# Prompt attention of a streaming encoder step: values as the stationary operand, two heads side by side, and the reciprocal row sums put into the transposition

## The reference

```python
admissible = key_chunk[None, :] <= (pb // CHUNK)[:, None]          # CHUNK = 64
score = jnp.einsum('bth,bths->bts', wb.astype(F32), jax.nn.relu(dots))
sel_val, sel_idx = lax.top_k(jnp.where(admissible[None], score, -jnp.inf), n_sel)   # 256 keys
...
logits = jnp.einsum('btkgd,btskd->btkgs', qg, kg, preferred_element_type=F32) * scale
logits = jnp.where(valid[:, :, None, None, :], logits, -jnp.inf)
p = jax.nn.softmax(logits, axis=-1).astype(vg.dtype)
o = jnp.einsum('btkgs,btskd->btkgd', p, vg)
```

## Time and profile before

| | us |
|---|---|
| median of 3 runs | 4250.42 |
| lowest and highest run | 4244.04, 4252.89 |
| span of the profiled execution | 4256.5 |
| prompt attention in it, first row maximum to last output | 646.3 |
| of this, tiles 0 to 3 | 207.0 |
| of this, tiles 4 to 7 and the end | 439.3 |

### The profile page before, as it was taken

How to read it: one execution, slowest core, us unless ns; L and a number is a source line. 1 busy time by engine, 2 the same in 40 slices (tenths; PEclk the granted TensorE clock), 3 DMA queues, 4 the chain that set the end, 5 groups by cost and what they waited for, 6 DMA issues and landing times. The chain is left out here.

```text
span 4256.5 us, 57639 instructions
## 1 busy us (share of the span) xinstructions
PE 3965.5 (93%) x20761; PEld 3571.6 (84%) x20777; DVE 2283.6 (54%) x3818; ACT 1126.7 (26%) x2017; POOL 220.7 (5%) x300
## 2 busy tenths in 40 slices
PE   6999999987999999979978899999888899999998
PEld 5988888876999999969963678888447799999997
DVE  5455555545444444454477888877223444444445
ACT  4322222213111111122133433333332311112111
POOL 2000000003000000020000000000000200000000
PEclk8888888869999999999958555555999999999999
DMA  2111011001111111111212000000431011111111
GB/s 85 36 36 36 32 36 37 31 11 42 40 45 36 50 40 40 42 42 66 74 44 84 16 6 6 1 1 1 175 148 40 27 40 45 45 36 46 40 45 57
DMA packets 58083, 187.32 MB, mean 44 GB/s; under 512 B 6960, under 2 KB 23344, under 8 KB 53488
## 3 DMA queue, kind: packets, MB, share of 16 engines
q1 hardware_dynamic: 53184, 165.22, 11.2%
q0 software_dynamic: 4656, 18.65, 1.4%
HBM read 164.28 MB, written 19.57 MB: 43 GB/s over the span
## 5 line engine op out<-in xcount | busy, mean ns | idle before, releaser
L205 PE MATMUL ff0lin<-ff0h_hi,ff0w_hi 128*128 128x384 f32 x1056 | 356.1, 337 | 23.7 <-POOL ff0h_lo L163 15.4
L205 PE MATMUL ff1lin<-ff1h_hi,ff1w_hi 128*128 128x384 f32 x1056 | 356.7, 338 | 21.7 <-POOL ff1h_lo L163 13.8
L206 PE MATMUL ff1lin<-ff1h_lo,ff1w_hi 128*128 128x384 f32 x1056 | 356.1, 337 | 0.0
L207 PE MATMUL ff1lin<-ff1h_hi,ff1w_lo 128*128 128x384 f32 x1056 | 355.6, 337 | 0.0
L206 PE MATMUL ff0lin<-ff0h_lo,ff0w_hi 128*128 128x384 f32 x1056 | 355.2, 336 | 0.0
L207 PE MATMUL ff0lin<-ff0h_hi,ff0w_lo 128*128 128x384 f32 x1056 | 354.8, 336 | 0.0
L1643 PEld LDWEIGHTS ap_bank<-at_v,ap_probs_t 128*128 128x128 f32 x1152 | 258.6, 331 | 36.4 <-ACT ap_probs_t L1688 20.4
L205 PE MATMUL hg_lin<-hg_h_hi,hg_w_hi 128*128 128x384 f32 x768 | 271.1, 353 | 16.1 <-POOL hg_h_lo L163 14.2
L1643 PE MATMUL ap_bank<-at_v,ap_probs_t 128*128 128x64 f32 x1152 | 269.1, 418 | 10.2 <-ACT ap_probs_t L1688 10.1
L206 PE MATMUL hg_lin<-hg_h_lo,hg_w_hi 128*128 128x384 f32 x768 | 265.0, 345 | 0.0
L207 PE MATMUL hg_lin<-hg_h_hi,hg_w_lo 128*128 128x384 f32 x768 | 264.4, 344 | 0.0
(11 more groups left out here) (328 smaller groups left out, 8767.4 us busy)
## 6 DMA issues: line engine op xcount, KB each, us to landing
ff0raw<-in_weights SPq DMA_DIRECT2D x66, 512.0 KB, 3.3
ff1raw<-in_weights SPq DMA_DIRECT2D x66, 512.0 KB, 3.2
hg_raw<-in_weights SPq DMA_DIRECT2D x40, 512.0 KB, 3.3
as_keys<-in_cache_k SPq DMA_DIRECT2D x16, 1024.0 KB, 4.8
as_vals<-in_cache_v SPq DMA_DIRECT2D x8, 2048.0 KB, 9.2
pj_raw<-in_weights SPq DMA_DIRECT2D x18, 512.0 KB, 3.9
se_keys<-in_cache_ki SPq DMA_DIRECT2D x8, 1024.0 KB, 4.7
x<-in_x SPq DMA_DIRECT2D x3, 1536.0 KB, 7.1
```

The lines of the kernel that those rows point to most:

```text
L205: pe.matmul(out, w_hi, x_hi, start=start, stop=False)
L206: pe.matmul(out, w_hi, x_lo, start=False, stop=False)
L207: return pe.matmul(out, w_lo, x_hi, start=False, stop=stop)
```

## The change

The two heads of a block become one unit, and the pipeline has one more stage. Per unit:

- Scores: the products of the two heads alternate, so that neighbours use partitions 0 to 63 and 64 to 127. For tiles 4 to 7 the second piece of keys stands behind the first half's transposition of the unit before.
- q is negated when it is projected and the mask is +1e30, so VectorE takes a minimum, and the exponential has scale -1; the negation (L1754) is gone. The minima of both heads are joined in one instruction.
- The row sums of both heads are inverted in one instruction, and it now stands behind the unit's top steps instead of ahead of them.
- GpSimd multiplies the identity by the two columns of reciprocals (`diag`, new, 128 x 256). The transposition becomes a float32 product with `probs` stationary and `diag` moving, which transposes and scales at once.
- Values: V (64 columns) is stationary, `probs_t` (128 columns) moving. The two heads write partitions 0 to 63 and 64 to 127 of one bank. The output comes out transposed, so L1649, `o` and L1702 are gone, and one copy of 128 x 128 per unit is left.
- `probs` and `probs_t` hold two units, q has one buffer. In `attend_sample_phase` the negation of the maximum and the drain ahead of it are gone.

```diff
-NEG = -1e30
+NEG = 1e30
...
-                    copy_rows(m * 2 + (Q_SLAB + par), m * 2 + (FIRST_Q + par), 1 - par, HEAD_D ** -0.5)
+                    copy_rows(m * 2 + (Q_SLAB + par), m * 2 + (FIRST_Q + par), 1 - par, -HEAD_D ** -0.5)
...
+            def diagonal(n):
+                pool.wait_ge(inv_set, n + 1)
+                if n >= 2:
+                    pool.wait_ge(turned, 2 * parts_before[n - 1])
+                pool.tensor_tensor(diag[:, n % 2], spread(const["ident"][:, :].unsqueeze(1), [P, 2, P]),
+                                   spread(inv[:, n % 2], [P, 2, P]), ALU.mult).then_inc(diag_set, 1)
+            split_lo(0)
+            for n in range(n_units):
+                if n % QB == QB // 2 and n // QB + 1 < PT:
+                    split_lo(n // QB + 1)
+                diagonal(n)
...
         @block.tensor
+            def scores(n, c):
+                t, j = units[n]
+                if c >= len(parts[n]):
+                    return
+                if j == 0 and c == 0:
                     pe.wait_ge(q_lo_set, t + 1)
                 if n:
-                    pe.wait_ge(maxed, 2 * n + half - 1)
-                for c, (a, e) in enumerate(pieces((t + 1) * P)):
-                    out, keys = qk[half][c][:, 0:e - a], (rows, j // GROUP, slice(a, e))
-                    pe.matmul(out, q_hi[rows, t % 2, j, :], k_hi[keys], start=True, stop=False)
-                    pe.matmul(out, q_lo[rows, t % 2, j, :], k_hi[keys], start=False, stop=False)
-                    i = pe.matmul(out, q_hi[rows, t % 2, j, :], k_lo[keys], start=False, stop=True)
+                    pe.wait_ge(read, parts_before[n - 1] + min(c + 1, len(parts[n - 1])))
+                a, e = parts[n][c]
+                for q_part, k_part in ((q_hi, k_hi), (q_lo, k_hi), (q_hi, k_lo)):
+                    for half in range(2):
+                        rows = slice(half * HEAD_D, (half + 1) * HEAD_D)
+                        i = pe.matmul(qk[half][c][:, 0:e - a], q_part[rows, t % 2, j, :], k_part[rows, j // GROUP, a:e],
+                                      start=q_part is q_hi and k_part is k_hi, stop=k_part is k_lo)
                 i.then_inc(qk_done, 1)
             def turn(n, half):
-                t, j = blocks[n]
-                pe.wait_ge(exped, 2 * n + half + 1)
-                if n or half:
-                    pe.wait_ge(turned_out, 2 * n + half)
+                pe.wait_ge(diag_set, n + 1)
+                for c, (a, e) in enumerate(parts[n]):
+                    m = turn_no(n, half, c)
+                    if m >= 2:
+                        pe.wait_ge(turned_out, m - 1)
+                    for k in range(a // P, e // P):
+                        i = pe.matmul(tr[m % 2][:, (k * P - a):(k * P - a) + P], probs[:, n % 2, half, k * P:(k + 1) * P],
+                                      diag[:, n % 2, half, :], start=True, stop=True)
+                    i.then_inc(turned, 1)
+            def values(n):
+                t, j = units[n]
+                pe.wait_ge(turned_out, 2 * parts_before[n + 1])
+                if n >= 2:
+                    pe.wait_ge(o_out, n - 1)
+                out = ob[n % 2]
                 for c in range(t + 1):
-                    i = pe.transpose(tr[c // 4][:, c % 4 * P:(c % 4 + 1) * P], probs[:, half, c * P:(c + 1) * P], const["ident"][:, :])
-                i.then_inc(turned, 1)
...
+                    for half in range(2):
+                        col = (j // GROUP * 2 + half) * HEAD_D
+                        i = pe.matmul(out[half * HEAD_D:(half + 1) * HEAD_D, 0:P], v_sb[:, c, col:col + HEAD_D],
+                                      probs_t[:, n % 2, half, c * P:(c + 1) * P], start=c == 0, stop=c == t)
                 i.then_inc(pv_done, 1)
...
+            for n in range(n_units + 2):
+                if n < n_units:
+                    scores(n, 0)
+                if 0 <= n - 1 < n_units:
+                    turn(n - 1, 0)
+                if n < n_units:
+                    scores(n, 1)
+                if 0 <= n - 1 < n_units:
+                    turn(n - 1, 1)
+                if n >= 2:
+                    values(n - 2)
...
+                act.activation(probs[:, n % 2, half, 0:keys], probs[:, n % 2, half, 0:keys], ACT.Exp, bias=low[:, n % 2, half],
+                               scale=-1.0, accum_out=total[:, n % 2, half]).then_inc(exped, 1)
+                act.activation(o_t[:, j, t * P:(t + 1) * P], ob[n % 2][:, 0:P], ACT.Copy).then_inc(o_out, 1)
...
+            def invert(n):
+                dve.wait_ge(exped, 2 * n + 2)
+                if n >= 2:
+                    dve.wait_ge(diag_set, n - 1)
+                dve.reciprocal(inv[:, n % 2], total[:, n % 2]).then_inc(inv_set, 1)
+            def minima(n):
+                t = units[n][0]
+                one = len(parts[n]) == 1
+                if n >= 2:
+                    dve.wait_ge(turned, 2 * parts_before[n - 1])
+                for c, (a, e) in enumerate(parts[n]):
+                    dve.wait_ge(qk_done, parts_before[n] + c + 1)
+                    for half in range(2):
+                        i = dve.tensor_tensor_reduce(out=probs[:, n % 2, half, a:e], in0=qk[half][c][:, 0:e - a],
+                                                     in1=mask_p[:, mask_at(t) + a:mask_at(t) + e], scale=1.0, scalar=3e38,
+                                                     op0=ALU.add, op1=ALU.min,
+                                                     accum_out=low[:, n % 2, half] if one else part_min[:, n % 2, c, half:half + 1])
+                    i.then_inc(read, 1)
+                if one:
+                    dve.drain().then_inc(low_set, 1)
+                else:
                     dve.drain()
...
+                    dve.tensor_tensor(low[:, n % 2], part_min[:, n % 2, 0].unsqueeze(2), part_min[:, n % 2, 1].unsqueeze(2),
+                                      ALU.min).then_inc(low_set, 1)
+            for n in range(n_units):
+                minima(n)
+                take_top(steps_by[n - 1] if n else first_steps, steps_by[n])
+                invert(n)
...
-                dve.reduce_max(neg_max[:, p], part_max[:, p, :], AX.X)
-                dve.drain()
-                dve.tensor_scalar(neg_max[:, p], neg_max[:, p], -1.0, None, ALU.mult).then_inc(maxed, 1)
+                dve.tensor_reduce(low[:, p], part_min[:, p, :], AX.X, ALU.min).then_inc(maxed, 1)
```

170 lines of the change are left out of this document (59 added, 111 removed).

## The result

| | before | after |
|---|---|---|
| median of 7 runs, us | 4250.12 (4244.04 to 4253.5) | 4260.07 (4258.17 to 4264.79) |
| ratio | | 1.0027 [1.0016, 1.0038] |
| span of the profiled execution, us | 4256.5 | 4256.6 |
| first load of the prompt attention to first load of the sample attention, us | 657.6 | 669.5 |
| sample attention, us | 247.1 | 243.5 |

The kernel is 10 us slower. In the profiled executions the prompt attention is 11.9 us longer. That the two spans are equal all the same comes from 4.6 us less ahead of it and 3.7 us less behind the sample attention, where the code is the same, and 3.6 us less in the sample attention. So single stages are compared from here on, and whole kernels by their medians.

What follows compares the result with a forecast made beforehand. TensorE was taken to bound the kernel before, a cross-engine chain in tiles 4 to 7 after. 184 + 469 + 10 = 663 us against 646.3 gave a 4267 us median; forecast bounds 4259 to 4290, range 4195 to 4310.

Steps and rivals of the forecast that it cites:

- TensorE bounds before, the chain after: Late tiles: TensorE sets the pace before; afterwards reciprocal, diagonal, first half's transposition, second piece's scores, 4.4 to 6.3 us a unit.
- Waits in tiles 4 to 7: VectorE idles for second-piece scores 3.1, 3.5, 4.3, 5.0 us a unit by tile, eight units each: 127 us.
- rival 3: Tiles 4 to 7: part of the chain at full clock, 19 us come back, 4248 us, no change; chance 0.16.
- Transposition: two records of 0.213 for 128 keys: TensorE at the low clock: transposing by product doubles from 0.213 to 0.427 us per 128 keys, 123 us more.
- Pairs side by side: TensorE: two heads' products run at once; values 0.427 us per chunk instead of 0.87, score pairs 0.43 instead of 0.85.
- rival 2: Prompt attention: the heads do not run side by side, +77 us on the forecast, 4344 us; chance 0.15.
- VectorE's own work: Tiles 4 to 7: 346.3 us falls to 326 without negations, joins and reciprocals; tiles 0 to 3: 176.4 to 161.
- Tiles 0 to 3: Early tiles, one piece: VectorE waits for nothing; 161 work, 19 gaps, 4 first units, 184 us against 207.0.
- Tail: After the last top step: diagonal, 16 transposing products, copies and values, about 10 us.
- Sum: Prompt attention: 184 + 469 + 10 = 663 us against 646.3, +17; kernel median 4267 us.
- Rival 1, the full clock in the chain: Tiles 4 to 7: chain at 2.4 GHz saves 66 us there, kernel 4193 us, or 4230 with half; chance 0.27.
- The prediction's sign, a clock of 0.50 at the start of each transposition: Tiles 4 to 7: granted clock 0.50 whenever a transposition starts; the prediction is wrong if it is 1.00 there.

Runs made afterwards that it cites:

- e1_scores_first: Changed kernel with both pieces' scores of a unit placed ahead of both transpositions of the unit before: 4149.97 us, 0.9768 of the kernel before.
- e6_recip_early: Changed kernel with the reciprocals in the middle of a unit's top steps instead of behind them: 4152.11 us, 0.9768 of the kernel before.
- e3_diag_twice: Changed kernel with the GpSimd diagonal multiply done once more per unit, into a spare tile: 4285.77 us, 1.0087 of the kernel before.
- e10_same_rows: Changed kernel with both heads' score products on partitions 0 to 63: 4283.86 us, 1.0087 of the kernel before.
- e11_same_columns: Changed kernel with values head after head, both heads writing partitions 0 to 63 and the output copied in two pieces: 4272.84 us, one run.
- e5_filler: Changed kernel with 4 x t extra TensorE products of constants behind each unit's values in tiles 4 to 7: 4223.72 us, 0.9935 of the kernel before.
- e2_heads_apart: Changed kernel with a piece's score products ordered three of one head, then three of the other: 4265.84 us, 1.0038 of the kernel before.
- e9_values_apart: Changed kernel with the value products of all chunks of one head ahead of those of the other: 4267.19 us, one run.
- e4_plain_transposes: Changed kernel with plain transposes against the identity in place of products with the diagonal, division left out: 4218.13 us, 0.9928 of the kernel before.

## Why the prediction came out right, step by step

Forecast 4267, measured 4260.07, inside the forecast's own bounds (4259 to 4290), 1 us from their fast end. It is slower than before, by 0.23% of the medians; the interval, 0.16 to 0.38%, leaves out no change, but not the 0.2% that the prediction took as its limit. The mechanism was right; that the number fell inside those narrow bounds is in part luck, as the terms show.

- **TensorE bounds before, the chain after.** Held. The change takes 225 us of work off TensorE and loses them to a chain through VectorE, GpSimd and TensorE; e1_scores_first, e6_recip_early and e3_diag_twice move that chain alone and move the time by what they do to the waits.
- **Waits in tiles 4 to 7: forecast 127 us, measured 110.2.** By tile 3.1, 3.5, 4.3, 5.0 against 2.2, 3.3, 3.9, 4.4. The diagonal took 0.61 us where I took 0.7, which is 3 us of 17. In tile 7 the chain of the unit shown is 5.93 against 6.3: 0.91 to the transposition (forecast 1.05), 3.71 for it (3.41) and 1.31 for the scores (1.85), whose last two pairs ran at the full clock. In tile 4 the cause is the clock at the start of the chain: five of its eight units began the transposition at the full clock and waited 1.4 to 2.4 us. A unit of tile 4 wholly at the low clock, the first of the two shown above, waited 2.84; eight such would wait 22.7 us, and 17.3 were measured. So both halves of rival 3 are in the result in part: the clock rose before the scores ended in tile 7, and it still held from the burst before in tile 4. Together they are worth less than the 19 us that the rival gave them, since the waits as a whole are 17 short.
- **Transposition: two records of 0.213 for 128 keys.** Held: 16 records in 3.78 us, (3.78 - 0.42) / 15 = 0.224.
- **Pairs side by side.** Held for scores and values; rival 2 is refuted by e10_same_rows for the scores (worth 24 us) and by e11_same_columns for the values. The forecast of rival 2, +77, also counted TensorE as its own bound in tiles 2, 3 and 7, at the low clock throughout.
- **VectorE's own work: forecast 326, measured 331.6 in tiles 4 to 7; 161 and 167.3 in tiles 0 to 3.** This step was off by 12 us. I took off each removed instruction at its full length. In tiles 4 to 7 the lengths of all records together did fall by 19.7, as forecast (20). But short instructions overlap their neighbours in the records, and the busy time, which counts an overlap once, fell by 14.6; in tiles 0 to 3 by 9.1, where 15.1 was forecast and the lengths fell by 13.6. The half of the earlier trace rows shows it, with the reciprocal at 2804.65 between these two lines:

```profile
2804.54 0.15 DVE L1754 TENSOR_SCALAR ap_neg_max<-ap_part_max 128x1 f32<-128x1 f32 x1
...
2804.73 2.29 DVE L1341 MAX8 se_top<-score_s 128x8 f32<-128x2064 f32 x1
```

Negation and reciprocal last 0.15 and 0.16 us, but are 0.10 and 0.08 from the start of the next. In tiles 4 to 7 the gaps between instructions made up for most of the error: about 12 us, forecast 16.
- **Tiles 0 to 3: forecast 184, measured 193.2.** VectorE is busy for 0.87 of it, as forecast (over 0.85). 6 us are the step just named. The other 3 are idleness: tile 0 needs 29.7 us for eight units, at clock 0.50 as its row shows, and there the reciprocals wait for the exponentials (7.9 us in tiles 0 to 3). I had given the first units 4 us.
- **Tail: forecast 10, measured 11.3** from the last reciprocal (2973.45) to the start of the last copy (2984.77): the 32 transposing records ran at the low clock but for the last few (6.73 us), the values at the full one.
- **Sum.** Tiles 0 to 3 came out 9 us longer than forecast and tiles 4 to 7 with the tail 14 us shorter (465.0 against 479: own work +5.6, waits -16.8, gaps -4, tail +1.3): +11.9 in the phase instead of +16.7. The two errors are of opposite sign, and the total is better than its terms. That is luck: with the waits alone as they came out, the forecast would have been 4250, no change.
- **Rival 1, the full clock in the chain**, was priced at 66 us for the waits, and e5_filler, which brings it about in most units, takes 51.2 off the waits for piece two and puts 8.7 ahead of piece one. The prediction's sign, a clock of 0.50 at the start of each transposition, held in 26 of the 32 units, all of tiles 6 and 7 among them, where TensorE idles for 4.8 to 7.8 us before it. It did not in five units of tile 4 and one of tile 5, after idleness of 2.5 to 4.4 us.

## What to carry to other kernels

Work taken from the engine that bounds a kernel buys nothing if the same edit puts that engine's next input behind a round trip over two others: ask of each queued group what it waits for, and put ahead of it whatever the other engines need sooner. Here the same instructions in another order are 2.6% faster (4149.97 against 4260.07). Start a cross-engine round trip (here one reciprocal of 0.17 us) while its engine still has independent work queued, and the length of the trip, even a transposition at double price, no longer counts.

## What the runs showed of the hardware

- TensorE runs two products side by side that use different partitions, also when they are not neighbours in the program: three of one head ahead of three of the other ran in pairs (e2_heads_apart). With 16 ahead, nearly nothing of the overlap was left (e9_values_apart, 3.33 us against 1.97 in alternation and 3.71 with none).
- Products that share rows but write different columns overlap as well: 32 records of 128 moving columns in 1.97 us, 0.055 a record, against (3.71 - 0.28) / 31 = 0.111 on the same columns.
- More work can make TensorE's part shorter: with 1408 more records (165.7 us busy) the granted clock between 2530 and 2930 rose from 0.75 to 0.98, 2.4 GHz nearly throughout, and the kernel lost 36 us.
- What kept the clock at 0.50 all through the phase before, with TensorE busy nearly throughout, is not settled. None of the new forms alone is needed for the higher clock. Not the product in place of the transpose: with plain transposes (e4_plain_transposes) the clock between 2530 and 2930 is 0.72, with products 0.75. Not scores side by side: on the same rows (e10_same_rows) it is 0.73, and with the values on the same columns (e11_same_columns) 0.80. The Trainium skill, "TensorE: Matmul & The Clock Gate", Part 4, says that transpose mode does not count as busy for the clock; no run here shows a difference that it would make, and in e4_plain_transposes a group of 8 plain transposes ran at the full clock (1.10 us at 2872.30, against 1.97 at the low one). The old form of the values, 64 moving columns, was put back in no run.
